# Splitting the last down tile by token half, with the latents' norm beside its second half, and GpSimd taking six weight splits

## The reference, cut to what matters

```python
h = _rms(x, norm2_g[i]) * (1.0 + sc2) + sh2
x = x + g2 * _swiglu(h, ffn_w_gate[i], ffn_w_up[i], ffn_w_down[i])      # the same for the context y
...
h = _rms(x, norm1_g[i]) * (1.0 + sc1) + sh1                             # layer 1: norm number 2 of the kernel
hc = _rms(y, norm1_g[i]) * (1.0 + csc1) + csh1
q, k, v = split(h @ w_in)                                               # od_in: 1024 x 3072
qc, kc, vc = split(hc @ w_in)
q, k = _rms(q, q_g), _rms(k, k_g)                                       # per head of 64
```

## Time and profile before

| | us |
|---|---|
| median of 3 runs | 2134.99 (2134.18 to 2138.87) |
| the profiled execution | 2134.16 |
| its span | 2132.3 |
| PE busy in the span | 2070.2 (97%) |
| DVE busy | 1499.5 (70%) |
| ACT busy | 975.3 (46%) |
| POOL busy | 325.4 (15%) |

### The profile page before, as it was taken

One profiled execution on the slowest core, in us unless ns is written; L12 is line 12 of the kernel. 1 busy time (PEld: TensorE's weight loads), 2 busy tenths in 40 slices (PEclk: granted clock), 3 DMA queues, 4 the chain that ended last, 5 costly groups with the idle time before them and its releaser, 6 DMA issues.

```text
span 2132.3 us, 34735 instructions
## 1 busy us (share of the span) xinstructions
PE 2070.2 (97%) x12633; PEld 1770.0 (83%) x12633; DVE 1499.5 (70%) x2685; ACT 975.3 (46%) x1545; POOL 325.4 (15%) x340
## 2 busy tenths in 40 slices
PE   7999999999989998999999999999999999999998
PEld 3756778888878768999999989999988888888887
DVE  5535578894247855665687867997986677777776
ACT  3436332222234365444478534447743444444444
POOL 0114000000004031000000016887820000000000
PEclk9999999999999999999999999999999999999999
DMA  8351245694226303555545544551156655555553
GB/s 294 118 210 69 99 158 194 214 325 136 96 79 179 99 11 110 186 180 188 181 160 165 174 159 136 172 169 60 60 184 221 198 187 188 190 191 189 187 188 117
DMA packets 92896, 342.18 MB, mean 160 GB/s; under 512 B 10383, under 2 KB 10399, under 8 KB 92272
## 3 DMA queue, kind: packets, MB, share of 16 engines
q1 hardware_dynamic: 89280, 325.10, 45.5%
q0 software_dynamic: 3504, 15.56, 2.5%
HBM read 339.57 MB, written 1.05 MB: 160 GB/s over the span
## 4 chain that ended last, share of the span: by engine, by line
PE 91%; DVE 4%; ACT 2%; issue 1%; DMA 1%; POOL 1%; SPq 0%; DVEq 0%; ACTq 0%; POOLq 0%
PE banks L1077 20%; PE banks L1514 16%; PE banks L1126 9%; PE banks L1480 7%; PE banks L1392 6%; PE banks L1263 5%; PE banks L1483 3%; PE banks L1441 3%; PE banks L975 2%; PE banks L1425 2%; PE banks L1091 2%; PE banks L1165 2%; PE banks L957 1%; PE banks L1004 1%; PE banks L1018 1%
## 5 line engine op out<-in xcount | busy, mean ns | idle before, releaser
L1077 PE MATMUL banks<-act_parts,first_w_parts 128*128 128x512 f32 (+1 forms) x2544 | 464.4, 344 | 3.1 <-DVE ffn_hidden_parts L2121 1.7
L1077 PEld LDWEIGHTS banks<-act_parts,first_w_parts 128*128 128x128 f32 x2544 | 400.9, 190 | 63.9 <-issue 7.3
L1514 PE MATMUL banks<-w_parts,a_parts 128*128 128x512 f32 x1524 | 360.4, 390 | 0.1
L2121 DVE TENSOR_TENSOR first_w_parts<-weight_ring,first_w_parts 128x1024 fp32r<-128x1024 f32 x166 | 206.8, 1248 | 202.1 <-ACT first_w_parts L1708 202.0
L1514 PEld LDWEIGHTS banks<-w_parts,a_parts 128*128 128x128 f32 x1524 | 285.9, 188 | 59.5 <-issue 0.8
L2121 DVE TENSOR_TENSOR w_parts<-weight_ring,w_parts 128x1024 fp32r<-128x1024 f32 x207 | 253.7, 1226 | 74.3 <-ACT w_parts L1708 71.7
L1708 ACT ACTIVATE w_parts<-weight_ring 128x1024 fp32r<-128x1024 f32 x207 | 218.9, 1057 | 184.0 <-PE banks L1480 102.1
L1708 ACT ACTIVATE first_w_parts<-weight_ring 128x1024 fp32r<-128x1024 f32 x166 | 174.8, 1056 | 237.2 <-PE banks L1077 124.0
L1480 PE MATMUL banks<-n_parts,w_parts 128*128 128x512 f32 x632 | 229.4, 397 | 1.3 <-DVE w_parts L2121 1.3
L1126 PE MATMUL banks<-ffn_hidden_parts,first_w_parts 128*128 128x512 f32 (+1 forms) x1056 | 183.4, 336 | 0.0
L1126 PEld LDWEIGHTS banks<-ffn_hidden_parts,first_w_parts 128*128 128x128 f32 x1056 | 162.6, 190 | 20.5
(11 more groups left out here) (327 smaller groups left out, 2904.0 us busy)
## 6 DMA issues: line engine op xcount, KB each, us to landing
weight_ring<-in_stream SPq DMA_DIRECT2D x618, 512.0 KB, 3.3
main_zone<-in_rel_bias POOLq DMA_DIRECT2D x6, 512.0 KB, 11.7
rounded<-in_dft_input POOLq DMA_DIRECT2D x1, 1600.0 KB, 7.5
rounded<-in_dft_inverse POOLq DMA_DIRECT2D x1, 1280.0 KB, 7.8
main_zone<-in_xT POOLq DMA_DIRECT2D x1, 1024.0 KB, 11.5
main_zone<-in_ctxT POOLq DMA_DIRECT2D x1, 1024.0 KB, 16.2
main_zone<-in_c_rows POOLq DMA_DIRECT2D x1, 1024.0 KB, 8.4
tail_zone<-in_rel_bias POOLq DMA_DIRECT2D x2, 512.0 KB, 23.6
```

Source lines behind the costliest of these rows:

```text
L1077: mm = pe.matmul(o[:, 0:w], wb[:, hw, k, :], fin[:, hx, k, 0:w], start=(k == 0 and n == 0), stop=(k == DC - 1 and n == 2))
L1514: mm = pe.matmul(acc[n][:, :], ap_[:, e % 3, ha, (n // 2) * P:(n // 2 + 1) * P], wp[(B + b) % PARTS][:, hw, (n % 2) * 512:(n % 2 + 1) * 51 ...
L2121: return dve.tensor_tensor(o, a, b, op)
```

## The change

1. The last of the 8 down tiles of layer 0 is done as two tiles of 256 columns, latents first (`down_last`; `ffn_d0` now counts 9 tiles, and every later tile number is one higher). Squares of blocks 0 to 6 are summed ahead of it and in it. In the second half PE also sums the last latents' squares and spreads their reciprocal, and ScalarE and VectorE do the latents' part of norm 2 (`norm_latents`).
2. The context's part of norm 2 is done inside `qk_norm` and among ScalarE's steps 0 to 5 of `od_in`. PE waits for it at tile 8.
3. The low parts of `od_in` blocks 3 to 8 are made by GpSimd (`POOL_LOW`), which loads and masks the bias after that and after the context's norm.
4. In both attentions the chunks of the first output tile stand ahead of the transposings of the step, and more of them.

The diff, cut to its core (`nth(k)` only renumbers the counts of norms behind number 2):

```diff
-TILES = [("ev_in", 10), ("ev_out", 8), ("ffn_gu0", 2 * FC), ("ffn_d0", 8), ("od_in", 16), ("od_out", 8),
+TILES = [("ev_in", 10), ("ev_out", 8), ("ffn_gu0", 2 * FC), ("ffn_d0", 9), ("od_in", 16), ("od_out", 8),
...
+        POOL_LOW = range(3, 9)
+        CONTEXT_HIGH = {0: (0,), 1: (1,), 2: (2,), 3: (3,), 4: (4, 5), 5: (6, 7)}
+        CONTEXT_LOW = {3: ((0, None),), 4: ((1, 0), (2, 1)), 5: ((3, 2),), 6: ((4, 3),), 7: ((5, 4), (6, 5)), 8: ((7, 6), (None, 7))}
...
+            def down_last():
+                name, m = "ffn_d0", DC - 1
+                pe.wait_ge(mod_used, len(MODS))
+                for c in range(DC - 2):
+                    add_squares(2, c)
+                o = bank_of(TILE[name] + m)
+                for k in range(FC):
...
+                        mm = pe.matmul(o[:, 0:L], wb[:, hw, b % 8, :], fhid[:, hx, k, 0:L],
+                                       start=(k == 0 and n == 0), stop=(k == FC - 1 and n == 2))
+                    if k == 11:
+                        add_squares(2, DC - 2)
+                mm.then_inc(tile_ready, 1)
+                o = bank_of(TILE[name] + DC)
+                for k in range(FC):
...
+                        mm = pe.matmul(o[:, L:T], wb[:, hw, b % 8, :], fhid[:, hx, k, L:T],
+                                       start=(k == 0 and n == 0), stop=(k == FC - 1 and n == 2))
+                        if b % 8 == 0 and n == 0:
+                            mm.then_inc(parts_begun, 1)
+                    if k == 5:
+                        pe.wait_ge(squares_ready, squared(2, DC - 2) + 1)
+                        add_last_squares((0, 1))
+                    if k == 10:
+                        pe.wait_ge(rstd_ready, 3)
+                        spread_half(0)
+                mm.then_inc(tile_ready, 1)
...
+                    if i >= PAIRS:
+                        out_part(l, AHEAD_OF_VALUES[l][i - PAIRS])
                     if 0 <= i - 2 < PAIRS:
                         turn(i - 2)
-                    if i >= PAIRS:
-                        out_part(l, AHEAD_OF_VALUES[l][i - PAIRS])
...
-            AHEAD_OF_VALUES = [[(0,), (1,), (2,)], [(0,), (1, 2), (3,)]]
+            AHEAD_OF_VALUES = [[(0,), (1, 2), (3, 4)], [(0,), (1, 2, 3), (4, 5)]]
...
                 if l == 0:
-                    norm(2)
-                    spread_rstd(2)
+                    down_last()
...
             split_first("od_in", L, 2)
+            pe.wait_ge(rstd_ready, 4)
+            spread_half(1)
             for j in range(2, 16):
+                if j == 8:
+                    pe.wait_ge(normed, DC * nth(2) + DC)
                 split_tile("od_in", j, L if j < 8 else T)
...
             for j in range(16):
                 project_in(1, "od_in", j, 0)
                 if j >= 2:
                     qk_root(1, j - 2)
+                for c in CONTEXT_HIGH.get(j, ()):
+                    high_half(1, c)
...
+            def scaled_half(s, c):
+                a, b, _ = halves(T)[s]
+                if c == 0:
+                    dve.wait_ge(rstd_spread, 3 + s)
+                stt(raw[:, c, a:b], X[:, c, a:b], GA[:, 1, 0, c, s:s + 1], bank[[5, 3][s]][:, a:b],
+                    ALU.mult, ALU.mult).then_inc(scaled_ready, 1)
+            def low_half(s, c):
+                a, b, _ = halves(T)[s]
+                dve.wait_ge(fin_hi, DC * (2 + s) + c + 1)
+                stt(fin[:, 1, c, a:b], raw[:, c, a:b], MOD[:, 1, c, s:s + 1], fin[:, 0, c, a:b].bitcast(F32),
+                    ALU.add, ALU.subtract).then_inc(normed, 1)
...
                     while split < min(count - l, first + j + lag + PARTS + 1):
-                        low(name, split)
+                        if l == 0 or split not in POOL_LOW:
+                            if l == 1 and split == POOL_LOW[-1] + 1:
+                                dve.wait_ge(w_lo, ORD[name] + split)
+                            low(name, split)
+                        if l == 1:
+                            for above, below in CONTEXT_LOW.get(split, ()):
+                                if above is not None:
+                                    scaled_half(1, above)
+                                if below is not None:
+                                    low_half(1, below)
...
-            evacuated(pool, "ffn_d0", DC)
-            pool.wait_ge(normed, DC * 3)
+            pool.wait_ge(w_lo, ORD["od_in"] + POOL_LOW[0])
+            for b in POOL_LOW:
+                s, n = SLOTS["od_in"][b], ORD["od_in"] + b
+                pool.wait_ge(w_hi, n + 1)
+                w = fwp[n % PARTS]
+                pool.tensor_tensor(w[:, 1, :], slot(s), w[:, 0, :].bitcast(F32), ALU.subtract).then_inc(w_lo, 1)
+            evacuated(pool, "ffn_d0", DC + 1)
+            pool.wait_ge(normed, DC * nth(2) + DC)
             pool.dma_start(mask_o, t["mask_odd"][:, :]).then_inc(bias_in, 16)
```

More of the change, by code:

```diff
@@ L603, in squared, with nth @@
         def squared(k, c):
-            return sum(DC if j in BEFORE else 1 for j in range(k)) + (c + 1 if k in BEFORE else 1)
+            return sum(DC if j in BEFORE else 1 for j in range(k)) + (c + 1 if k in BEFORE else 1) + ((k, c) >= (2, DC - 1))
+        def nth(k):
+            return k + (k >= 2)
         def halves(n):
@@ L829, in norm, with add_last_squares, spread_half @@
                     add_squares(k, c)
+            def add_last_squares(strips):
+                d = norms[2]
+                w = T // 4
+                for j in strips:
+                    mm = pe.matmul(bank[6][32 * j:32 * j + 32, 0:w], ones[:, 0:32], d["sq"][:, DC - 1, j * w:(j + 1) * w],
+                                   start=False, stop=True)
+                mm.then_inc(sumsq_ready, 1)
+            def spread_half(s):
+                w = T // 4
+                r = slice(64 * s, 64 * s + 64)
+                for j in (2 * s, 2 * s + 1):
+                    mm = pe.matmul(bank[[5, 3][s]][:, j * w:(j + 1) * w], small("strip")[r, j:j + 1].broadcast_to([64, P]),
+                                   rstd[r, 0:w], start=True, stop=True)
+                mm.then_inc(rstd_spread, 1)
@@ L1116, in down @@
                 name = f"ffn_d{l}"
-                for m in range(DC):
+                for m in range(DC - 1 + l):
                     o = bank_of(TILE[name] + m)
@@ L1750, in ffn @@
                     if l == 0:
-                        if m == DC - 1:
-                            for b in range(PARTS - 1):
-                                high("od_in", b)
-                        square(2, m)
+                        if m < DC - 1:
+                            square(2, m)
                     else:
@@ L2241, in norm, with last_half, turned_half, norm_latents @@
                         low_part(c - 1)
-                    if k == 2 and c == 5:
-                        low("od_in", PARTS - 1)
                 low_part(DC - 1)
+            def last_half(s):
+                m = DC - 1
+                a, b, _ = halves(T)[s]
+                o = tile("ffn_d0", m + s)[:, a:b]
+                stt(X[:, m, a:b], o, MOD[:, 0, 40 + m, s:s + 1], X[:, m, a:b], ALU.mult,
+                    ALU.add).then_inc(tile_free, 1)
+            def turned_half(s):
+                w = T // 4
+                r = slice(64 * s, 64 * s + 64)
+                dve.wait_ge(std_ready, 3 + s)
+                dve.reciprocal(rstd[r, 0:w], rstd[r, 0:w]).then_inc(rstd_ready, 1)
+            def scaled_half(s, c):
+                a, b, _ = halves(T)[s]
+                if c == 0:
[3 more added lines that the diff above has]
+            def low_half(s, c):
+                a, b, _ = halves(T)[s]
+                dve.wait_ge(fin_hi, DC * (2 + s) + c + 1)
+                stt(fin[:, 1, c, a:b], raw[:, c, a:b], MOD[:, 1, c, s:s + 1], fin[:, 0, c, a:b].bitcast(F32),
+                    ALU.add, ALU.subtract).then_inc(normed, 1)
+            def norm_latents():
+                last_half(0)
+                turned_half(0)
+                low("od_in", 0)
+                for c in range(DC):
+                    scaled_half(0, c)
+                    if c >= 1:
+                        low_half(0, c - 1)
+                    if c == 1:
+                        low("od_in", 1)
+                    if c == 4:
+                        last_half(1)
+                    if c == 6:
+                        low("od_in", 2)
+                low_half(0, DC - 1)
+                turned_half(1)
             def tile(name, j):
@@ L2413, in ffn @@
                     if l == 0 and m == DC - 1:
-                        for n in range(PARTS - 1):
-                            low("od_in", n)
+                        return
                     if l == 1 and m == DC - 1:
@@ L2486, in _ @@
             ffn(0, T)
-            norm(2)
+            norm_latents()
             qk_norm(1)
```

70 lines of the change are left out of this document (53 added, 17 removed).

## The result

| | before | after |
|---|---|---|
| median of 9 runs, us | 2136.59 (2133.77 to 2139.2) | 2143.56 (2140.93 to 2147.68) |
| ratio to before, 95% interval | | 1.003 (1.0022 to 1.0038) |
| span of the profiled execution, us | 2132.3 | 2145.1 |
| PE busy / DVE busy, us | 2070.2 / 1499.5 | 2080.7 / 1504.8 |

**7.0 us slower**, by the interval 4.7 to 8.1. I had forecast +0.5, with 2141.0 as the upper end: the prediction was wrong, and the time lies beyond the rival that I had priced on the slow side (2141.4). Of the 2.6 us past the upper end, 1.6 are that the kernel before has a median of 2136.59 in nine runs, where the prediction stood on 2134.99 in three; the other 1.0 is past it by the difference as well (+7.0 against +6.0).

What follows compares the result with a forecast made beforehand. PE, busy 97% of the span, was taken as the bound, with VectorE nearly full beside the query tiles. The terms -7.6 + 6.4 + 0.7 + 1.7 - 0.7 = +0.5 gave 2135.5 us; 8-in-10 range 2128.5 to 2141.0.

Steps and rivals of the forecast that it cites:

- the rival that I had priced on the slow side: "the masks catch PE twice", the slower case, priced at 2141.4 us; chance 0.14.
- Part 1: Last down tile in halves with the latents' norm inside: tile 2 of `od_in` starts 7.6 us earlier, bounds -9.0 and -6.0.
- Part 2: Context norm and GpSimd splits beside the query tiles: held VectorE operations and ScalarE waits cost +6.4 us, bounds 2.6 and 9.0.
- the 4.3: In Part 2, PE's wait in us after tile 6 for ScalarE's square of tile 5 and root of tile 3.
- the 2.1 after tile 7: In Part 2, PE's wait of 2.1 us after tile 7 for ScalarE's root of tile 4.
- My 2.6 for ScalarE's waits alone: In Part 2, the cost in us of ScalarE's waits without any holding-up, the lower bound.
- Part 3: At `v_by_token`, tile numbers one higher make PE wait for the tile just ended: +0.7 us, between 0 and 1.2.
- Part 4: Bias masks now run beside key tiles, where VectorE has less idle time: +1.7 us, between 0 and +3.4.
- Part 5: Chunks ahead of the transposings fill PE's waits for GpSimd's probabilities in the attentions: -0.7 us, between -1.1 and 0.
- the masks catch PE twice: Rival: masks start at about 685, two successive key tiles' low parts wait; +7.6 for 1.7, total 2141.4 us; chance 0.14.
- the gain stays: Rival: GpSimd's splits fall beside reciprocals, ScalarE's waits cost 2.6, masks nothing more; sum -5.0, 2130.0 us; chance 0.25.

Runs made afterwards that it cites:

- run 5: The kernel of run 2 with 28 matmuls, their results unread, filling PE's pause of 3.76 us after tile 6; 2135.07 us, ratio 0.9992.
- run 6: The kernel of run 2 with each of GpSimd's six splits cut into four pieces; 2132.56 us, ratio 0.9982.
- run 3: The changed kernel with ScalarE's high parts of context blocks 5 to 7 one step later and VectorE's low parts after them; 2144.86 us, ratio 1.0041.
- run 7: The kernel of run 6 with ScalarE's high parts of context blocks 5 to 7 one step later as well; 2133.94 us, ratio 0.9987.
- run 2: The changed kernel with each of the four mask operations cut into four pieces; 2134.46 us, ratio 0.9988.
- run 11: The kernel before with only its four mask operations cut into four; 2136.70 us, ratio 0.9996.
- run 1: The changed kernel with the tails of both attentions in the order of before; 2141.68 us, ratio 1.0022.
- run 4: The changed kernel with the six low parts back on VectorE, GpSimd only loading and masking the bias; 2145.51 us, ratio 1.0046.
- run 8: The kernel of run 2 with the tails of both attentions as before; 2134.13 us, ratio 0.9989.
- run 10: The kernel of run 9 with the tails of both attentions as before; 2129.52 us, ratio 0.9969.
- run 12: The kernel before with only the chunks ahead of the transposings, and more of them; 2137.11 us, ratio 1.0004.
- run 9: The kernel of run 7 with VectorE's last two context low parts ahead of tile 4's reciprocal and block 9's low part; 2129.26 us, ratio 0.9966.

## Why the prediction was wrong

- **Part 1** (-7.6): right, -7.3 measured; the waits inside `split_first` (0.21, 0.56, 0.61) sum to 1.4 where I had 1.8. One reading of before was wrong without harm to this sum: of the 20.7 us I put 11.7 down to waits. PE's marked waits there (1.48, 2.91, 0.60, 1.73, 0.61) are 7.3; most of the rest is PE at work at the lower clock. 24 matmuls took 5.61 behind the wait of 2.91, and the same 24 take 3.21 after the change. The view of busy time by stretch of the kernel before has the clock:

```profile
630.00:640.00 10.00, 6.91 (x37) 5.72 (x37) 9.82 (x24) 4.84 (x11) 0.00 (x0) 0.84 0.16 52
640.00:645.00 5.00, 5.00 (x32) 4.97 (x32) 2.00 (x3) 3.10 (x6) 4.22 (x7) 0.70 0.49 106
```

So what a pause of PE costs behind it stood in the rows of before, and I didn't carry it over to the pauses that I forecast.

- **Part 2** (+6.4): near in size, +5.9, and right in its rows (ScalarE's three waits, PE's 3.76 for the 4.3). What it lacked is the clock: the 2.1 after tile 7 came as a slow tile instead, which run 5 turned back into a wait of 1.63. The two are near in size, so that the sum holds without this step is partly luck. As to causes, the holding-up and ScalarE's order work together: with the first taken away 3.8 are left, with the second 2.3, with both 0.1 (runs 6, 3 and 7, to the sum after tile 7). My 2.6 for ScalarE's waits alone was low: run 6, with hardly anything held, has 3.8.
- **Part 3** (+0.7): right. The first value matmul starts 1.34 after the last sum of squares (714.39 and 715.73 in run 2), in run 11, with the tile numbers of before, 0.46: +0.9.
- **Part 4** (+1.7, bounds 0 to 3.4) **is the step that failed.** It measured 7.1 - 0.9 = +6.2, which is 4.5 of the 6.5 us between forecast and result, and run 2 gives back 7.8 by cutting the masks alone (more than the 6.2, since the 1.33 of before goes too). Its mechanism was right, and so was its place (masks at 697.43, which is 691.6 with the 5.9 taken off by which this execution lies later at the last down tile; forecast 685 to 705). Two things were wrong in its size: 3.8 of the 6.2 are waits, where the forecast had 1.7 and 3.4 as the worst case, and 2.4 are the clock. First, the waits. I priced a step with both two-input operations held at 9.5 and took the middle over where in a step the first mask falls. The steps measured 14.0 and 10.6 here, against PE's 6.3 each, so VectorE fell 12 us behind, not 6.5. The first mask fell at the worst point, 0.02 ahead of the scaling, but bad luck is not the whole of it. In run 3 it fell beside the reciprocal (696.25, the reciprocal from 695.73), and the steps still took 11.1 and 10.5. Second, the clock. PE at rest for 3.4 us then ran tile 14 at half clock, 2.4 more, no part of any term. The other traces with whole masks bear out both, by the same reckoning (a slow tile is its length by starts less the 5.87 of the others, the waits are what is left; run 3 also without the 2.2 of its slow tile 8):

| with whole masks | waits, us | slow tile, us | sum |
|---|---|---|---|
| changed | 3.8 | 2.4 | 6.2 |
| run 1 | 3.5 | 2.6 | 6.1 |
| run 3 | 3.7 | 2.0 | 5.7 |
| run 4 | 2.2 | 1.2 | 3.4 |

The waits alone lie above 1.7 in all four, and a slow tile stands behind them each time. My rival "the masks catch PE twice" had the event right, two waits in succession, and its price, 7.6, was nearer than the forecast's; the trigger that I gave it, transfers that end early and masks at 685, did not come, and wasn't needed. A chance of 0.14 was too low, as I read it now: four masks lie end to end for 20 us, over three of PE's steps, so two steps in succession were likely to be caught.
- **Part 5** (-0.7): nothing that can be measured (runs 8, 10 and 12). By the trace of run 12 -0.6 in the first attention (194.09 to 209.45 for 193.05 to 208.97) and +0.2 in the second (803.96 to 815.95 for 802.90 to 814.71). In the changed kernel's own trace the first was 0.6 longer than before, with a lower clock (last section).
- Of the 7.0, the stages account for 5.7. What the other 1.3 are stays open, all the more as the runs with small masks have no such rest; the spread of single runs of one kernel is 5 to 7 us.

The range was too narrow on the slow side: it took the bounds of Part 4 from steps and waits alone, and the steps too short. The rival "the gain stays" had -5.0; run 9 shows that it was to be had, with another order and GpSimd's operations in pieces.

## What to carry to other kernels

When work moves to GpSimd beside a busy VectorE, count not its total but the length of its longest operation: in this kernel each VectorE operation with both inputs in SBUF may stand behind one whole, and the remedy is to cut GpSimd's operations into pieces (with sixteen masks of 1.6 us PE waited for no low part, and the stage was 7.8 us shorter than with four of 5.0). The remedy pays where the stage has no slack: the kernel before gained nothing clear by it (run 11). When a step is issued later than before, look at the slack of the stage in which it lands, and price the worst phase, not the middle one. When the forecast has PE stand still, look in the trace of before at what a like pause did to the matmuls behind it. A gain in one stage has to be followed to the next: with the pieces small, ScalarE's parts behind the data that they need and the last parts ahead of the reciprocal, the 7.3 us reached the end.

## What the hardware did that I had not expected

PE's granted clock fell from 1.00 to 0.50 in the pauses of 3.76 and 3.38 us, and the tile behind each took 5.27 for 3.22 and 8.44 for 6.03; after pauses of 1.30 and 2.06 (run 6) the next tiles took 3.21 and 5.82, as always. It does not go by the length of one pause alone. Before the change, the clock was at 0.70 from 640 to 645 us though no single wait just ahead of it was over 1.73. The same pause of 0.97 in the first attention was followed by full speed in one execution and by slow matmuls in another, of the changed kernel (0.94 in place of 0.66 for four matmuls), where the row of that stretch shows 0.61:

```profile
198.00:200.00 2.00, 1.78 (x12) 1.26 (x12) 0.67 (x7) 0.81 (x2) 1.46 (x3) 0.61 0.58 213
```

And a slow tile need not cost its own length: where a chain of other engines sets the pace, filling the pause kept the clock up, won only 0.7 us of 2.2 in its stage, and nothing in the time of the kernel.
